# Trainium2 decoder trunk: split-weight regions moved apart in SBUF, and each slot given its own start offset

## What is computed

```python
for l in range(2):
    h = rms_norm(x, mix_norm[l]); z = h @ w_in[l]          # 1024 x 5632
    ...                                                     # S5 scan, differential attention
    m = sigmoid(g_ssm) * (y_a @ w_proj_ssm[l]) + sigmoid(g_attn) * (y_b @ w_proj_attn[l])
    x = x + m @ w_out[l]
    h = rms_norm(x, ffn_norm[l])
    x = x + (swiglu(h, ...) if l == 0 else moe_swiglu(h, ...))   # D_FF 2816; top 2 of 8 experts
return rms_norm(x, final_norm)
```

## Time and profile before

| what | us |
|---|---|
| median of the two runs (1454.07 and 1454.91) | 1454.49 |
| span of the profiled execution, first to last instruction | 1453.1 |

### The profile page before, as it was taken

The page is one execution under the profiler, slowest core; times in us unless marked ns, Lnnn a source line. Parts: engine busy times, 40 slices in busy tenths (PEclk is TensorE's granted clock), DMA queues, the critical chain, the costliest instruction groups (busy, mean ns, idle before and its releaser), DMA issues.

```text
span 1453.1 us, 22261 instructions
## 1 busy us (share of the span) xinstructions
PE 1426.3 (98%) x8381; PEld 1202.9 (83%) x8381; DVE 1179.7 (81%) x1181; ACT 884.7 (61%) x879; POOL 141.4 (10%) x195
## 2 busy tenths in 40 slices
PE   8999999999999999999999999999999999999997
PEld 6887888999998888887888888888888888888875
DVE  7998886676467697876988988889898898898896
ACT  5334754534344345644768768777777777777774
POOL 1910100000000000101960000000000000000100
PEclk9999999999999999999999999999999999999999
DMA  7443445776455442454999999999999999999993
GB/s 285 136 180 121 156 159 189 261 246 233 151 189 192 174 160 97 151 188 161 365 413 390 406 363 399 380 364 413 353 398 394 354 404 370 379 397 347 419 376 145
DMA packets 94247, 408.87 MB, mean 281 GB/s; under 512 B 28769, under 2 KB 43233, under 8 KB 47714
## 3 DMA queue, kind: packets, MB, share of 16 engines
q1 hardware_dynamic: 75984, 391.37, 69.9%
q10 hardware_dynamic: 17042, 12.36, 2.6%
q0 software_dynamic: 1152, 4.19, 0.7%
HBM read 390.98 MB, written 14.16 MB: 279 GB/s over the span
## 4 chain that ended last, share of the span: by engine, by line
PE 78%; DVE 11%; DMA 3%; SPq 3%; issue 2%; ACT 2%; POOL 1%; DVEq 0%; POOLq 0%; ACTq 0%
PE psum L1938 25%; PE psum L1940 24%; PE psum L1939 24%; DVE w_lo L605 4%; SPq L696 3%; PE psum L1954 2%; DMA w_raw<-in_stream 2%; DMA x_normed<-y_rows,row_number 1%; ACT w_hi L599 1%; ACT square_out L993 0%; PE psum L2284 0%; PE psum L2005 0%; DVE s_r L1511 0%; ACT prob L1129 0%; PE psum L1987 0%
## 5 line engine op out<-in xcount | busy, mean ns | idle before, releaser
L605 DVE TENSOR_TENSOR w_lo<-w_raw,w_hi 128x2048 fp32r<-128x2048 f32 x267 | 607.9, 2293 | 130.2 <-ACT w_hi L599 129.4
L599 ACT ACTIVATE w_hi<-w_raw 128x2048 fp32r<-128x2048 f32 x267 | 509.4, 1915 | 251.1 <-PE psum L1940 191.5
L1938 PE MATMUL psum<-w_hi,hsT_hi 128*128 128x512 f32 x448 | 176.0, 393 | 0.8 <-DVE hsT_lo L1829 0.8
L1940 PE MATMUL psum<-w_lo,hsT_hi 128*128 128x512 f32 x448 | 174.5, 390 | 0.0
L1939 PE MATMUL psum<-w_hi,hsT_lo 128*128 128x512 f32 x448 | 174.3, 389 | 0.0
L1938 PE MATMUL psum<-w_hi,hT_hi 128*128 128x512 f32 x376 | 152.7, 406 | 1.8 <-ACT gate_ssm L1075 1.4
L605 DVE TENSOR_TENSOR w_lo_more<-w_raw,w_hi_more 128x2048 fp32r<-128x2048 f32 x56 | 128.2, 2289 | 24.3 <-ACT w_hi_more L599 23.6
L1940 PE MATMUL psum<-w_lo,hT_hi 128*128 128x512 f32 x376 | 147.4, 392 | 0.0
L1939 PE MATMUL psum<-w_hi,hT_lo 128*128 128x512 f32 x376 | 147.1, 391 | 0.0
L599 ACT ACTIVATE w_hi_more<-w_raw 128x2048 fp32r<-128x2048 f32 x56 | 107.1, 1913 | 21.6 <-DMA w_raw<-in_stream 12.4
L1938 PE MATMUL psum<-hT_hi,w_hi 128*128 128x256 f32 x416 | 116.6, 280 | 0.2 <-DVE hT_lo L1463 0.2
(11 more groups left out here) (429 smaller groups left out, 2651.2 us busy)
## 6 DMA issues: line engine op xcount, KB each, us to landing
w_raw<-in_stream SPq DMA_DIRECT2D x323, 1024.0 KB, 6.9
w_raw_more<-in_stream SPq DMA_DIRECT2D x40, 1024.0 KB, 7.7
h_rows<-one_row ACTq DMA_DIRECT2D x10, 512.0 KB, 6.6
round_rows<-h_rows SPq DMA_DIRECT2D x7, 512.0 KB, 7.0
y_rows<-y_slots ACTq DMA_DIRECT2D x7, 512.0 KB, 9.2
y_rows<-one_row ACTq DMA_DIRECT2D x4, 512.0 KB, 6.2
gain_row<-in_gain_rows SPq DMA_DIRECT2D x3, 512.0 KB
x_tok<-in_x SPq DMA_DIRECT2D x2, 512.0 KB, 6.2
```

Of the source, the lines that this page charges most:

```text
L599: nc.scalar.activation(split_of(seg, i)[0], raw_of(seg, i), ACT.Copy).then_inc(s_hi, 1)
L605: nc.vector.tensor_tensor(l_, raw_of(seg, i), h.bitcast(F32), ALU.subtract).then_inc(s_lo, 1)
L1938: mm(out, lh, rh, start=start, stop=False)
L1940: return mm(out, lh, rl, start=False, stop=stop)
```

## The change

Regions of `w_hi` and `w_lo` come to lie 2,176 elements (8,704 bytes) apart in place of 2,048. Every slot gets an offset in its region: in the dense segment one of eleven, by the block j of the slot (in bytes 0, 64, 128, 192, 256, 320, 384, 448, 32, 96, 224 for j = 0 to 10; gate, up and down slot of a block alike), in the mixer of layer 0 320 bytes, in that of layer 1 192 bytes, in the rounds 320 bytes for the three regions. The two more places of the rounds are left as they are. `w_hi` and `w_lo` grow by 1,280 bytes each; for that `o_square_out` is laid over the area of `s5_decay` and `rope_cos` is allocated later. The tiles behind `w_lo`, `ident` first, move with its end.

```diff
-LEAD = 48
+WIDE = 2176
+LEADS = (0, 16, 32, 48, 64, 80, 96, 112, 8, 24, 56)
+MIX_LEAD = (80, 48)
+ROUND_LEAD = 80
...
-        wh = sb("w_hi", [P, NW * SLOT + LEAD], F32R)
+        wh = sb("w_hi", [P, 2 * WIDE + SLOT + 112], F32R)
         here[0] += (a_hT - here[0]) % 512
-        wl = sb("w_lo", [P, NW * SLOT + LEAD], F32R)
+        wl = sb("w_lo", [P, 2 * WIDE + SLOT + 112], F32R)
         ident = sb("ident", [P, P])
         identb = sb("identb", [P, P], BF16)
         maskb = sb("maskb", [P, P], BF16)
-        cosT = sb("rope_cos", [P, NT, 32])
...
-        osq = sb("o_square_out", [P, 256])
+        osq = at("o_square_out", [P, 256], F32, a_rr + 12288)
+        cosT = sb("rope_cos", [P, NT, 32])
...
-        def stationary(seg, i):
+        def lead(seg, i):
             if seg == 1:
-                return i % NW != 1 and FFN_SLOTS[i][0] != "d"
-            return False
+                return LEADS[FFN_SLOTS[i][1]]
+            return ROUND_LEAD if seg == 3 else MIX_LEAD[seg // 2]
...
             if p < NW:
-                a = (p + 2) % NW * SLOT + (LEAD if stationary(seg, i) else 0)
+                a = (p + 2) % NW * WIDE + lead(seg, i)
```

## The result

The kernel after takes 1464.87 us (median of 1464.56 and 1465.18) against 1454.49 us. It is slower by 10.4 us, 0.7% by these medians; the estimate of the ratio is 1.0079, 95% interval 1.0062 to 1.0096. The forecast was 8 us faster, the range 1425 to 1468: the time lies inside the range, on the wrong side of before.

What follows compares the result with a forecast made beforehand. The distance between TensorE's matmul starts was taken to bound the kernel. Moving weights 8.5 plus stationary mixer weights 0.6 less 1.1 for waits made 8.0 us less: span 1445.1, time 1446.5 us, range 1425 to 1468.

Steps and rivals of the forecast that it cites:

- What bounds the kernel: Whole kernel: the distance between TensorE's matmul starts sets the end; TensorE 1426.3 of 1453.1 us.
- Two of the signs that were named: Dense blocks in the timeline: block 0 near 120 ns between starts, block 3 near 117.7.
- the one on moving weights: Rounds, mixers, dense down: extra falls from 13.5 to 11.0 ns; 2.3 ns on 3,696 matmuls, 8.5 us less.
- the steps between settled values: All matmuls: steps the same for 256 and 512 columns, so the extra is a cost per hand-over, not per column.
- the two more places: Rounds: places whose offset the change leaves at 0, counted as untouched, with no term in the sum.
- The lock is lost: All touched places: the new offsets never settle, 232.2 ns a matmul, 20.0 us more plus 1.9, 1476 us; chance 0.20.
- Stationary weights in the mixers: Mixers: from 119.8 to 117.7 ns on 288 matmuls, 0.6 us less; ends 1.9 us less and 1.6 more.
- Dense gate and up: Dense segment, 1,056 stationary matmuls: eleven offsets replace one, taken as 0; ends -4.6 and 2.2 us.
- The spacing and the moved `ident`: Regions 8,704 bytes apart change nothing modulo 512; `ident` from 192 to 448, 3 us either way; both taken as 0.
- The splits: ScalarE and VectorE on the shifted regions: 0 us; a few per cent longer would still lie under TensorE's matmuls.
- That DMA would carry a faster round: Rounds: 4.6 us of 750 less needs 380 in place of 378 GB/s; DMA gave 419, so the gain passes through.
- start addresses don't matter: Skill's port rule gives a sum of 0; as rival for moving weights only: changes within 2 us, 1454 us, chance 0.29.

Runs made afterwards that it cites:

- e5: e4 with the rounds' stationary activations 64 bytes off and the three regions' moving weights at seven offsets by slot group; 1465.8 us beside 1451.3 before, single execution.
- e7: Same as e5 but with the activations at 192 bytes; 1463.0 us in a single execution, beside 1451.3 for before.
- e1: The kernel after with every offset 0, the 8,704-byte spacing and moved small tiles kept; ratio to before 1.0017 (1.0006 to 1.0028).
- e4: The kernel after with offset 320 bytes where weights are stationary and 0 where they move; 1451.84 us, ratio to before 0.9989.
- e9: e4 with dense gate and up at 192 bytes and 0 to 12 bf16 fillers ahead of blocks 2 to 10; 1454.5 us beside 1454.1 before, single execution.
- e11: e4 with the dense down slots at 192 bytes, gate and up at 320; 1447.7 us in a single execution, beside 1454.1 for before.
- e12: The same kernel as e11, timed against before in five executions; 1447.66 us, ratio 0.9964 (0.9951 to 0.9978).

## Why the prediction was wrong

**What bounds the kernel** was right. TensorE's starts set the end before and after, the extra per hand-over depends on the offsets, and the change, 10 us, came from it with no instruction added. Two of the signs that were named came true as well: dense block 0 is at 120.0 ns and block 3 at 117.7.

**The step that failed** is the one on moving weights: "What counts there can be the distance of the two operands modulo 512 bytes, and 320 bytes on the moving side is the same distance (0 - 320 = 192 modulo 512) as 192 on the stationary side. The extra would fall from 13.5 to 11.0". Half of it is true: the distance counts (e5 to e7). Modulo 256 the 320 of the rounds is 64, and weights stationary at 192 also make 64 (0 - 192 = 64 modulo 256), so for the 320 bytes even the equality held. But what a distance is worth depends on the columns: 64 shortens a 256-column hand-over from 120 to 117.7 or 113.3, and lengthens a 512-column one from 226.7 to 228.9. The sentence that I drew it from, that the steps between settled values are the same for 256 and 512 columns "as far as the rows tell", rested on the value at one offset, 0. And the argument was for 320 bytes only: I used its 2.3 ns also for mixer 1 at 192 bytes and for the eleven offsets of the down slots, which by my own rule are other distances (all but one of them), and which turned out the dearest. I took 2.3 ns less on 3,696 matmuls, 8.5 us; measured were 2.0 ns more in the rounds, 1.1 in mixer 0, 5.2 in mixer 1 and 3.9 in the down slots, together 9.5 us more.

**What the sum left out.** I counted the two more places as untouched. They lost 1.9 ns on each of 1,152 matmuls, 2.2 us, through the crossings. The cost of finding back stood in the earlier trace rows.

**The right rival** was the third, "The lock is lost", in its sign and about half its size. It wasn't an unsettled stream, though: at 320 and 192 the stream settles within a few matmuls, in a worse pattern (232, 226, 229) or at a worse value (233.3). That the range reached up to 1468 and so holds the time is owed to this rival alone, not to the sum. The chance of 0.20 that I gave it was small for a term whose own rows, as I wrote, showed offset 0 only.

**Smaller terms.** Stationary weights in the mixers: 0.6 us less foreseen; they fell by 5.8 and 1.9 ns on 144 each, 1.1 us. Dense gate and up: 0 foreseen, with ends -4.6 and 2.2; they rose by 0.8 ns on 1,056, 0.8 us. The spacing and the moved `ident`: 0 foreseen, nothing seen in e1 (192 and 448 bytes, the old and the new place of `ident`, are the same modulo 256). The splits: no change (VectorE's busy time above). That DMA would carry a faster round wasn't put to the test by this change; in no run did TensorE's rounds get shorter distances than before.

The Trainium skill ("SBUF — State Buffer", section "Who interferes with whom") gives TensorE two independent read ports and says that it never waits on anyone. Read as "start addresses don't matter", it would have given 1454 us. This case disagrees with that reading: e5 has 233.0 and 226.4 ns in one round, in slots that differ in 64 bytes of offset. Where inside TensorE or SBUF the time goes, no run shows.

**What stays open.** Why the number of columns turns the order of the distances round; and what of the entry picks 113.3 or 117.7. That the offset of a block alone doesn't decide it is shown by e4 beside after, by e9, and by e11 beside e12; the rule isn't known. A second, shorter value of 512-column streams at distance 0 was seen in none of the traces and wasn't searched for; at another distance e5 has two.

## What to carry to other kernels

When one matmul stream bounds a kernel, read the distance of its starts and not its busy share, and treat the start addresses of its two operands as a tuning parameter: the distance between moving and stationary operand modulo 256 bytes moved a float32 (fp32r) hand-over by up to 7 ns, 3 to 6% of the matmul. The best distance found for one shape says nothing of another shape; 512-column matmuls wanted 0, 256-column ones 64 or 192. Look at the granted clock of both executions before comparing spans. A map costs one run, by giving each stage of one kernel another offset and reading the timeline, and it should come before the change.

## What was not expected of the hardware

- Many of the settled distances share one step. 226.7 and 233.3 ns for 512 columns, 113.3 and 120.0 for 256, are 544, 560, 272 and 288 cycles at 2.4 GHz, all multiples of 16; 117.7 is a pattern of three steps with 848 cycles, again one (53 x 16). Others, 118.3 and 118.7 at 32, 96 and 384 bytes, repeat in longer patterns.
- A stream keeps its settled distance over 96 matmuls and from one slot to the next, and has two of them at one offset (e4, e9, e12; with 512 columns e5). A few bf16 fillers of 128 columns, 0.06 us each, ahead of a block can move its 96 matmuls from 117.7 to 113.3 (e9, four or eight of them).
- A change of distance in the middle of a stream costs for up to ten matmuls behind it, also in places that were not changed.
